# Chunked retention: the turned keys' PSUM slot is given back at once, normalizing goes behind the state steps, and attention begins without a barrier

## The reference

```python
def retention_dir(q, k, v, log_gamma, include_diag):      # q, k, v in chunks of 128
    ...
    s = einsum('bhncd,bhnkd->bhnck', q, k) * decay_in[:, None]
    o_in = einsum('bhnck,bhnke->bhnce', s, v)
    k_dec = k * exp(lg * (C - 1 - idx)...)
    kv = einsum('bhncd,bhnce->bhnde', k_dec, v)
    step: state, kv_n -> state * chunk_decay + kv_n       # scan over the chunks
    q_dec = q * exp(lg * (idx + 1.0)...)
    return o_in + einsum('bhncd,bhnde->bhnce', q_dec, s_prev)

def retention_branch(q, k, v, gate, log_decay, pad):
    ...                                                   # both directions, added
    o = (o - mean(o)) * rsqrt(var(o) + EPS)               # over each head's 128
    return o * silu(gate)

def attention_branch(q, k, v, sink, pad):
    ...                                                   # scores on the band and the meta keys
    p = softmax(concatenate([s_sink, s_meta, s_band]))
    return p[meta] @ meta_v + p[band] @ vband
```

## Time and profile before

| | us |
|---|---|
| median of 3 runs | 3866.2 (3865.33 to 3871.68) |
| profiled execution | 3871.39 |
| its span in the profile | 3869.6 |

### The profile page before, as it was taken

One profiled execution on the slowest core, in us unless ns is written; L12 is line 12 of the kernel. 1 busy time (PEld: TensorE's weight loads), 2 busy tenths in 40 slices (PEclk: granted clock), 3 DMA queues, 4 the chain that ended last, 5 costly groups with the idle time before them and its releaser, 6 DMA issues. The chain is left out here.

```text
span 3869.6 us, 55271 instructions
## 1 busy us (share of the span) xinstructions
PE 3669.0 (95%) x22252; PEld 3335.1 (86%) x22252; DVE 2249.2 (58%) x3881; ACT 1438.4 (37%) x2109; POOL 937.2 (24%) x792
## 2 busy tenths in 40 slices
PE   8978999999897999999899999999999999999998
PEld 7967899999796678788677886699999999999998
DVE  4434455554543545545557443347997886677775
ACT  3244444222324445322355343333333343333333
POOL 1000022112100002211103500017975673211110
PEclk9989999999998999999999999999999999999999
DMA  3111132222121123322221121236877999999994
GB/s 136 62 40 53 61 128 82 92 93 88 56 66 48 55 77 115 111 87 99 70 82 61 34 83 59 87 102 213 262 235 204 282 287 310 334 308 306 310 307 147
DMA packets 293613, 545.01 MB, mean 141 GB/s; under 512 B 138288, under 2 KB 187568, under 8 KB 292976
## 3 DMA queue, kind: packets, MB, share of 16 engines
q1 hardware_dynamic: 185248, 394.47, 31.7%
q0 software_dynamic: 27648, 100.68, 7.7%
q10 hardware_dynamic: 80464, 46.33, 4.0%
HBM read 484.03 MB, written 56.62 MB: 140 GB/s over the span
## 5 line engine op out<-in xcount | busy, mean ns | idle before, releaser
L304 PE MATMUL PSM<-UX,PARTS 128*128 128x264 f32 (+3 forms) x3392 | 1170.8, 345 | 55.1 <-DVE UX L333 24.9
L305 PE MATMUL PSM<-UX,PARTS 128*128 128x264 f32 (+3 forms) x3392 | 1149.2, 339 | 0.0
L306 PE MATMUL PSM<-UX,PARTS 128*128 128x264 f32 (+3 forms) x3392 | 1146.6, 338 | 0.0
L272 DVE TENSOR_TENSOR PARTS<-RAW,PARTS 128x1024 fp32r<-128x1024 f32 x549 | 687.8, 1259 | 540.4 <-ACT PARTS L262 538.5
L262 ACT ACTIVATE PARTS<-RAW 128x1024 fp32r<-128x1024 f32 x612 | 644.9, 1056 | 956.5 <-PE PSM L306 486.0
L304 PEld LDWEIGHTS PSM<-UX,PARTS 128*128 128x128 f32 x3392 | 645.3, 190 | 132.0 <-DVE UX L333 34.7
L305 PEld LDWEIGHTS PSM<-UX,PARTS 128*128 128x128 f32 x3392 | 645.8, 190 | 45.1 <-issue 2.6
L306 PEld LDWEIGHTS PSM<-UX,PARTS 128*128 128x128 f32 x3392 | 644.2, 190 | 44.9
L2827 PE MATMUL PSM<-AC,PARTS 128*128 128x416 f32 x1024 | 360.5, 352 | 4.0 <-DVE AC L3111 4.0
L2828 PE MATMUL PSM<-AC,PARTS 128*128 128x416 f32 x1024 | 359.7, 351 | 0.0
L2829 PE MATMUL PSM<-AC,PARTS 128*128 128x416 f32 x1024 | 359.5, 351 | 0.0
(11 more groups left out here) (437 smaller groups left out, 5500.5 us busy)
## 6 DMA issues: line engine op xcount, KB each, us to landing
RAW<-w_ff_dram SPq DMA_DIRECT2D x128, 512.0 KB
RAW<-peer_u_dram SPq DMA_DIRECT2D x128, 512.0 KB
RAW<-peer_v_dram SPq DMA_DIRECT2D x128, 512.0 KB
RAW<-w_in_dram SPq DMA_DIRECT2D x116, 512.0 KB
acts_dram<-MQ ACTq DMA_DIRECT2D x128, 208.0 KB
MQ<-acts_dram SPq DMA_DIRECT2D x128, 208.0 KB, 3.9
MQ<-gates_dram SPq DMA_DIRECT2D x128, 208.0 KB, 4.9
RAW<-w_mix_o_dram SPq DMA_DIRECT2D x32, 512.0 KB
```

What stands on the lines that cost most here:

```text
L272: e.tensor_tensor(p[:, 1024:2048], self.raw.of(i), p[:, 0:1024].bitcast(F), SUB).then_inc(V.sem, V.tick("w", i))
L304: e.matmul(dst, wh[k], xh_[k][:, lo:hi], start=(k == 0), stop=False, skip_group_check=True)
L305: e.matmul(dst, wh[k], xl_[k][:, lo:hi], start=False, stop=False, skip_group_check=True)
L306: m = e.matmul(dst, wl[k], xh_[k][:, lo:hi], start=False, stop=(k == kk - 1), skip_group_check=True)
```

## The change

It has five parts.

1. DVE gives the `kt` slot back before it waits for the pair's decay factors (in layer 0 behind the meta scores, which need them), and no longer has `normed` of the pair before in front of that.
2. ACT makes a pair's decay factors one pair ahead. The roots of both heads of a pair are taken together: one Ln table load, two Ln, one Exp table load, two Exp. `W.act(2a+3)` stands ahead of them.
3. On DVE the logs of the next pair stand before the state recurrence, and `normed` of the pair before behind it.
4. The fifth turn of the loop is gone. The last two variances are made by TensorE in step 0 of attention, behind its scores and its fill product. ACT takes their roots ahead of attention's first Exp, and DVE multiplies behind the first maximum.
5. The barrier on entering attention is gone. Meta queries, meta keys and the sinks' sums are made at the end of the stage before, POOL copies the first three sinks before the last two gated products, and the buffers are laid out so that attention's scores no longer share space with what the last pair's normalizing uses. Attention's outputs still share it, and wait for POOL's end of retention.

```diff
+        sd, sdm = [wk(512) for _ in range(2)], wk(32)
+        qdF, qdB, kdF, kdB = wk(512), wk(TT), wk(512), wk(512)
+        qm, sinks = wk(64), wk(16)
+        oP[0] = oX + 3248
         gx, sq2 = [wk(TT) for _ in range(3)], [wk(TT) for _ in range(2)]
...
+            if l == 0:
+                y = sinks[0:64, 0:8].rearrange("p (h a) -> p h a", h=2)
+                e.tensor_tensor(y, MH[0:64, oVec + 64:oVec + 72].rearrange("p (h a) -> p h a", h=2),
+                                con["sel"][0:64].unsqueeze(1).to_broadcast([64, 2, 4]), MUL).then_inc(V.sem, V.tick())
+                e.wait_ge(V.sem, V.n)
+                e.tensor_reduce(sinks[0:64, 8:10], y, AX.X, ADD).then_inc(V.sem, V.tick("sinks"))
             stage_end(V, ("in", l))
...
             if a < 4:
                 e.wait_ge(V.sem, V.at("logs", l, a))
+                if a >= 1:
+                    e.wait_ge(V.sem, V.at("qd", l, a - 1))
...
+            e.wait_ge(V.sem, V.at("rot", l, 12))
+            if l == 0:
+                e.tensor_copy(qm.rearrange("p (a c) -> p a c", a=4),
+                              QK[:, oQA:oQA + 4 * TT].rearrange("p (a c) -> p a c", a=4)[:, :, 0:16]).then_inc(
+                                  G.sem, G.tick("meta queries", l))
+            e.tensor_copy(kx[:, 528:544], kx[:, 0:16]).then_inc(G.sem, G.tick("meta keys", l))
             stage_end(G, ("in", l))
...
+        def variance_pe(e, l, h):
+            n = TT - 16 * l
+            b, back = ps.take("ss", ("ret", l, h))
+            for q, v in back:
+                e.wait_ge(q.sem, v)
+            e.wait_ge(S.sem, S.at("dev2", l, h))
+            gemm(e, b, [con["onesm"]], [sq2[h % 2][:, 0:n]], n).then_inc(T.sem, T.tick("var", ("ret", l, h)))
...
-            for a in range(5):
-                if a < 4:
+            for a in range(4):
...
                 if a >= 1:
-                    variance(2 * a - 2)
-                    variance(2 * a - 1)
-                if a < 4:
+                    variance_pe(e, l, 2 * a - 2)
+                    variance_pe(e, l, 2 * a - 1)
...
+        def roots_act(e, l, a):
+            n = TT - 16 * l
+            e.preload_act_table(ACT.Ln)
+            for h in (2 * a, 2 * a + 1):
+                tag, rs = ("ret", l, h), sq2[h % 2]
+                e.wait_ge(T.sem, T.at("var", tag))
+                e.activation(fv(rs[:, 0:n], n), pv(ps.of("ss", tag), n), ACT.Ln, bias=eps).then_inc(S.sem, S.tick())
+                ps.give(S, "ss", tag)
+            e.wait_ge(S.sem, S.n)
+            for h in (2 * a, 2 * a + 1):
+                rs = sq2[h % 2]
+                e.activation(rs[:, 0:n], rs[:, 0:n], ACT.Exp, scale=-0.5).then_inc(S.sem, S.tick("rstd", ("ret", l, h)))
...
-            for a in range(5):
+            for a in range(4):
+                W.act(e, first["fill", l] + 2 * a + 3)
                 if a >= 1:
-                    for h in (2 * a - 2, 2 * a - 1):
-                        rstd_act(e, ("ret", l, h), n, sq2[h % 2], 1.0, "var")
-                    e.wait_ge(V.sem, V.at("qd", l, a - 1))
-                    decays_act(e, l, a)
...
+                    roots_act(e, l, a - 1)
+                decays_act(e, l, a + 1)
...
+            roots_act(e, l, 3)
...
             def decays(a):
-                e.wait_ge(S.sem, S.at("decays", l, a))
                 if l == 0:
                     b = ps.of("kt", l, a)
+                    e.wait_ge(S.sem, S.at("decays", l, a))
...
                 ps.give(V, "kt", l, a)
+                e.wait_ge(S.sem, S.at("decays", l, a))
                 e.wait_ge(T.sem, T.at("score", l, a))
...
+            for a in range(4):
+                keys_decayed(a)
                 if a == 0:
                     centred_dve(e, l, 4)
+                decays(a)
+                queries_decayed(a)
+                logs_dve(e, l, a + 1)
+                states(a)
+                W.dve(e, first["fill", l] + 2 * a + 3)
                 if a >= 1:
-                    normed(2 * a - 2)
-                    normed(2 * a - 1)
+                    normed_dve(e, l, 2 * a - 2)
+                    normed_dve(e, l, 2 * a - 1)
+                W.dve(e, first["fill", l] + 2 * a + 4)
...
+                if h == 6:
+                    e.wait_ge(T.sem, T.at("ret", l, 3))
+                    for s in range(3):
+                        sink_pool(e, l, s)
...
                     scores(s)
                 for f in fill_at(l, s):
                     fill_pe(e, l, f)
+                if s == 0:
+                    variance_pe(e, l, 6)
+                    variance_pe(e, l, 7)
...
         def att_pool(e, l):
-            so = oVec + 64 + 8 * l
-            sink = MH[:, so:so + 8].rearrange("p (h a) -> p h a", h=2)
-            after_all(e, ("ret", l))
...
+            for s in range(3, len(steps(l))):
+                sink_pool(e, l, s)
...
-            after_all(e, ("ret", l))
...
+                if s == 0:
+                    normed_dve(e, l, 6)
+                    normed_dve(e, l, 7)
...
                     e.wait_ge(S.sem, S.at("oah", l, n))
+                    e.wait_ge(G.sem, G.at("end", ("ret", l)))
...
-            after_all(e, ("ret", l))
...
                     e.wait_ge(T.sem, T.at("ao", l, n, a))
+                    e.wait_ge(G.sem, G.at("end", ("ret", l)))
```

More of the change, by code:

```diff
@@ L438, in wk @@
             return WK[:, a:a + n]
+        sd, sdm = [wk(512) for _ in range(2)], wk(32)
+        qdF, qdB, kdF, kdB = wk(512), wk(TT), wk(512), wk(512)
+        qm, sinks = wk(64), wk(16)
+        oP[0] = oX + 3248
         gx, sq2 = [wk(TT) for _ in range(3)], [wk(TT) for _ in range(2)]
-        sd, sdm = [wk(512) for _ in range(2)], wk(32)
-        qdF, qdB, kdF, kdB, SF, SB = wk(512), wk(TT), wk(512), wk(512), wk(512), wk(512)
+        SF, SB = wk(512), wk(512)
         DT, PF, PB = wk(256), wk(128), wk(128)
@@ L452, in program @@
         pt_m = lambda half: WK[0:16, oX + 2448 + 256 * half:oX + 2704 + 256 * half]
-        tiny = [WK[:, oX + 2960 + i * 8:oX + 2960 + i * 8 + (8 if i < 3 else 16)] for i in range(4)]
+        tiny = [WK[:, oX + 2960 + i * 8:oX + 2968 + i * 8] for i in range(3)]
         oah = [OA[:, k * TT:k * TT + TT] for k in range(4)]
         oal = [OA[:, (4 + k) * TT:(4 + k) * TT + TT] for k in range(4)]
-        qm = WK[:, oX + 3008:oX + 3072]
         def out4(t, n):
@@ L787, in gate @@
                 tile_pe(e, ("g", l, h), i, W.both(i), us(c0, n), n)
-            for a in range(5):
-                if a < 4:
-                    keys_turned(a)
-                    scores(a)
+            for a in range(4):
+                keys_turned(a)
+                scores(a)
                 if a >= 1:
-                    variance(2 * a - 2)
-                    variance(2 * a - 1)
-                if a < 4:
[L797 to L800, removed]
-            stage_end(T, ("ret", l))
+                    variance_pe(e, l, 2 * a - 2)
+                    variance_pe(e, l, 2 * a - 1)
+                states(a)
+                gate(2 * a)
+                gate(2 * a + 1)
+                outputs(a)
+            stage_end(T, ("ret", l))
+        def roots_act(e, l, a):
[10 more added lines that the diff above has]
+                e.activation(rs[:, 0:n], rs[:, 0:n], ACT.Exp, scale=-0.5).then_inc(S.sem, S.tick("rstd", ("ret", l, h)))
         def ret_act(e, l):
@@ new lines, in ret_act @@
+                    roots_act(e, l, a - 1)
+                decays_act(e, l, a + 1)
+                for h in (2 * a, 2 * a + 1):
+                    W.act(e, first["fill", l] + h + 3)
+                    if h == 2 * a:
+                        e.preload_act_table(ACT.Silu)
+                    e.wait_ge(T.sem, T.at("g", l, h))
+                    if h >= 3:
+                        e.wait_ge(G.sem, G.at("gated", l, h - 3))
+                    e.activation(fv(gx[h % 3][:, 0:n], n), pv(ps.of("g", l, h), n), ACT.Silu).then_inc(
+                        S.sem, S.tick("g", l, h))
+                    ps.give(S, "g", l, h)
@@ new lines, in ret_act @@
+                for h in (2 * a, 2 * a + 1):
+                    b = ps.of("ret", l, h)
+                    o = flat[:, 512 * b + 1024 - n:512 * b + 1024]
+                    e.wait_ge(T.sem, T.at("ret", l, a))
+                    if h >= 2:
+                        e.wait_ge(V.sem, V.at("normed", l, h - 2))
+                    e.activation(sq2[h % 2][:, 0:n], o, ACT.Square).then_inc(S.sem, S.tick("dev2", l, h))
+                    e.activation(oS[h][:, 0:n], o, ACT.Copy).then_inc(S.sem, S.tick("o", l, h))
+                    ps.give(S, "ret", l, h)
@@ L905, in states, with normed_dve @@
                 ps.give(V, "kv", l, a)
[L907 to L914, removed]
+            for a in range(4):
+                keys_decayed(a)
                 if a == 0:
                     centred_dve(e, l, 4)
-                if a >= 1:
-                    normed(2 * a - 2)
-                    normed(2 * a - 1)
-                if a < 4:
-                    decays(a)
```

(18 more changed lines are left out.)

55 lines of the change are left out of this document (9 added, 46 removed).

## The result

| | us |
|---|---|
| before, median of 4 runs | 3868.94 (3865.33 to 3871.82) |
| changed, median of 4 runs | 3822.28 (3817.91 to 3823.8) |
| ratio | 0.9878, 95% interval 0.9861 to 0.9895 |
| profiled execution before, changed | 3871.39, 3822.32 |
| its span | 3869.6, 3820.5 |

The change is 1.2% faster. 3822.3 lies inside the range of 3803 to 3826, but 3.3 above the forecast's own range, and the forecast of 3812 was 10.3 too low.

The account below looks back on a forecast made before the run. TensorE bounds it, busy 3669.0 of 3869.6 us; only idle and slow clock can go. Terms -28.8 - 27.5 - 3.1 + 5.0 - 1.4 + 1.4 = -54.4 give 3812 from 3866.2; own range 3805 to 3819, wide 3803 to 3826.

Parts of the forecast that it names:

- Parts 1 to 3, retention: Pairs 1 to 3, both layers: stall and slow clock go, saving 28.8 and 27.5, in all 56.3 us.
- Part 4, start of attention in layer 0: Layer 0: step 1's scores 5.1 us sooner, about 2 of slow clock; net gain 3.1, between 2.5 and 5.1.
- The same in layer 1: Attention's start: second fill product 4.3 us later, plus 2 of slow clock; loss 5.0, between 3.3 and 5.6.
- The ring's turn: Attention's fill product 14: wait for the held slot goes in layer 0, comes in layer 1; -1.4 and +1.4 us.
- The sum: Whole kernel: retention, attention's start and ring terms together -54.4 us, giving 3812.
- wait moved inside the pair: Retention: slot on time but another link late, 2 us in each of six pairs; 3824, chance 0.08.
- the clock came back with the idle time: Rival for retention: clock stays low in parts, 43.0 instead of 56.3 us saved; 3825, chance 0.06.
- the weight tile was there: Rival at ScalarE's weight copy ahead of the roots: tile not loaded; 18 us late makes 3880, chance 0.02.
- no pause follows the table loads: Rival at attention's start: pause as long as the load, 1.28 us later twice; 3815, chance 0.02.

Follow-up runs that it names:

- The third experiment: Against the kernel before, in layer 1 only: the turned keys' slot given back directly behind the scaling of the keys; 3869.25 us, ratio 1.0004.
- The fourth: Against the changed kernel: VectorE's two products by the root put back between the turned keys and the meta scores; 3860.01 us.
- the repeat: The changed kernel run again without alteration, for a second profile; 3816.49 us.
- the roots one by one: Against the changed kernel: the two roots of a pair taken one after the other, adding two table loads per pair; 3821.2 us.
- the old tail: Against the changed kernel: last two variances, roots and products inside retention, barrier on entering attention and meta copies behind it again; 3808.3 us.
- the best kernel: Against the changed kernel: last two variances ahead of attention's first scores instead of behind its first fill product, still no barrier; 3797.51 us.
- work in both waits: Against the changed kernel: spare matmuls ahead of attention's first scores and 20 more behind the last variance; 3821.72 us.
- work in the first wait: Against the changed kernel: 4 (layer 1: 8) spare matmuls ahead of attention's first scores; 3820.87 us.

## Why the prediction was right, and where it was off

**Parts 1 to 3, retention: right.** Layer 0's three pairs took 71.9 us (274.57 less 202.68), forecast 72.15. Layer 1's took 65.3, forecast 65.7. They took 101.0 and 93.2 before, so the saving is 29.1 + 27.9 = 57.0, forecast 56.3. The stall and the slow clock behind it both went, and nothing took their place. Reading the price from whole pairs and not from the 43.0 of idle time was worth 13 us. One reading was loose: the prediction named the slot as what was 7 us late. The third experiment shows that the scores' slot came nearly as late, and its rows that the products and the decay factors, both behind the two roots, held it. The fourth shows that the early decay factors alone do not free it.

**Part 4, start of attention in layer 0: right kind, wrong size.** Forecast a gain of 3.1, measured 1.4 (step 2's scores 26.6 behind the last output, 28.0 before by the earlier trace rows). The scores of step 1 were forecast 16.2 behind the last output and stand at 17.1, because the first fill product took 7.5 us and not 6.0. Its clock had fallen behind waits of only 1.21 and 0.54. The second slow stretch cost 2.8 (scores and product 9.5 us for 6.66), forecast 2.0.

**The same in layer 1: right kind, wrong size.** The second fill product starts 20.1 us behind the last output (1221.06 less 1200.97), where it was 13.15 before. That is a loss of 6.9, forecast 5.0. At the third product it is 7.8, and at the fourth, where the kernel before waits 0.84 and the changed one does not, 6.9 again. The forecast's own working gives 4.3 + 2 - 0.8 = 5.5 and not the 5.0 that went into the sum. It had the second product at 17.4. Of the 2.7 more, 2.2 is the first product at 7.96 us instead of 5.8, behind a wait of 2.16, and 1.0 the scores before both products at half speed; the rest went 0.5 the other way. The prediction took this wait into its sum and not the slow clock behind it.

**The ring's turn: right.** Fill product 14 has no wait in layer 0, and in layer 1 the wait of 1.4 is there, at 1339.46. Behind it the clock is low for a few us, which the prediction did not price. But so it was behind the wait in layer 0 before (0.50 from 447.7 to 450.7), and the two cancel as the waits do:

```profile
1339.40:1342.40 3.00, 2.94 (x7) 2.37 (x8) 2.16 (x5) 2.91 (x6) 0.00 (x0) 0.50 0.01 3
```

**The sum.** From the profiled executions: -57.0 - 1.4 + 6.9 = -51.5, forecast -54.4. Measured is -49.1. The +2.4 between them stands elsewhere, where the program is the same. What differs there is above all where the clock is low: the changed kernel has one at 1520 (0.53 from 1519.5 to 1526.5) and one at 2151 that the kernel before has not, a longer one at 1844, and a shorter one at 2216. That these stretches make up the 2.4 is not shown. Further, the median of before was 2.7 higher than that of the three runs first shown, and medians differ by 46.7 where the profiled executions differ by 49.1. Together 10.3 = 3.6 (attention) - 0.7 (retention) + 2.4 (elsewhere) + 2.7 + 2.3 (the runs, with the forecast's rounding).

**The rivals.** None came true. No wait moved inside the pair, the clock came back with the idle time, the weight tile was there (ScalarE's copy at 204.78 follows at once), and no pause follows the table loads: 205.87 + 1.28 = 207.15, and the ACTIVATE starts at 207.17. So the drain of 1.38 us in the Trainium skill, "ScalarE: Activation LUTs", section "What ACT_TABLE_LOAD costs", is not seen here.

**What stays open.** Why the clock at the same places of the same program is low in one execution and not in another. The changed kernel shows it at its first fill product:

```profile
276.50:281.80 5.30, 5.26 (x43) 5.26 (x44) 0.45 (x1) 1.28 (x1) 0.00 (x0) 1.00 0.00 0
```

This is the repeat, behind the same waits as the 0.68 of the first profile. Four profiled executions have this start of attention unaltered as far as the first product (the changed kernel twice, the roots one by one, the normed products in front). In each layer the clock fell in three of the four. A term of this kind is worth 1.3 to 2.3 us in any one layer and execution, and no order of the work explains it.

## What to carry to other kernels

When a matmul waits for a PSUM slot, look at everything that stands ahead of the give-back, in the other engine's queue and in the queue that this one waits for in turn, and move all of it. Giving back sooner alone only moved the wait to the next slot here, and one of two late things moved alone won 12.9 of 57 us. Where a chain of another engine (variance, root, copy) must follow the last matmuls of a stage, put those matmuls ahead of the next independent product and not behind it: here that was worth 10.7 us in layer 0 and 10.4 in layer 1. Price a stall by the length of the whole stretch with and without it, and allow for a slow stretch behind short waits of 1 to 2 us too: here it came in six cases of eight.

## What the runs showed of the hardware

The granted clock fell to 0.50 not only behind the waits of 5 to 7 us but also behind 2.16 us (three executions of four), and behind 1.21 with 0.54 (three of four). It cost 1.5 us (layer 0) and 1.3 to 2.3 us (layer 1) in a fill product of 6.

Late in the program, far from the change, the same work at a clock of 1.00 goes at two speeds. First the profiled execution of the changed kernel, then its repeat, the same 200 us:

```profile
3300.00:3500.00 200.00, 200.00 (x1064) 198.96 (x1063) 142.27 (x170) 65.96 (x88) 33.72 (x36) 1.00 0.91 307
```

```profile
3300.00:3500.00 200.00, 200.00 (x1074) 199.55 (x1073) 144.30 (x172) 67.30 (x90) 35.60 (x38) 1.00 0.91 309
```

1064 matmuls against 1074 is 0.9%. From the first to the last matmul of L2852 it is 582.6 us against 576.4, of which a stretch of low clock at 3223, in the first execution alone, explains a part. Of the ten profiled executions seven ran at the lower speed (1063 or 1064: before, changed, the old tail, the best kernel, the early give, the roots one by one, work in both waits) and three at the higher (1073 or 1074: the repeat, work in the first wait, the normed products in front). In all seven the clock fell for some 3 to 7 us at the start of that stage, and in none of the three. That is a coincidence on record and not a cause. It doesn't touch the comparison of before and changed, whose profiled executions both ran at the lower speed. But these 6 us are over half of what the eight runs of the changed kernel differ by (3813.8 to 3823.8), and the cause isn't known.
